# Block 2 of a two-block kernel: attention's scratch memory taken apart from linear attention's, and its steps released earlier

## The reference, cut to what matters

```python
px, pc = split_cols(hx @ w_in + b_in), split_cols(hc @ w_in + b_in)   # tokens, context
ya_x = conv_module(*px[0:3], dw_w, dw_b, ln_g, ln_b, w_conv_out)      # 31 taps
yb_x, yb_c = gla_branch(px[3:9], pc[3:9], ..., need_ctx)              # gated linear attention
yc_x, yc_c = attn_branch(px[9:13], pc[9:13], q_norm_g, k_norm_g, w_attn_out, need_ctx)
xs = xs + gate_x * ((sigmoid(p[13]) * ya + sigmoid(p[14]) * yb + sigmoid(p[15]) * yc) @ w_out)

def gqa_attend(q, k, v):            # 8 query heads, 2 key heads, 64 wide
    s = einsum('bqkgd,bskd->bkgqs', q, k) * 64 ** -0.5
    return einsum('bkgqs,bskd->bqkgd', softmax(s, axis=-1), v)
```

## Time and profile before

| | |
|---|---|
| median of 3 runs | 1394.38 us |
| the profiled execution's own time | 1394.86 us |
| its span | 1393.5 us |
| PE busy | 1314.5 us (94%) |
| DVE busy | 870.2 us (62%) |
| ACT busy | 584.5 us (42%) |
| POOL busy | 281.6 us (20%) |
| chain that ended last: PE, DVE, issue, POOL | 74%, 10%, 10%, 4% |

### The profile page before, as it was taken

The page is one execution under the profiler, slowest core; times in us unless marked ns, Lnnn a source line. Parts: engine busy times, 40 slices in busy tenths (PEclk is TensorE's granted clock), DMA queues, the critical chain, the costliest instruction groups (busy, mean ns, idle before and its releaser), DMA issues.

```text
span 1393.5 us, 18891 instructions
## 1 busy us (share of the span) xinstructions
PE 1314.5 (94%) x7490; PEld 1037.0 (74%) x7490; DVE 870.2 (62%) x1496; ACT 584.5 (42%) x967; POOL 281.6 (20%) x217
## 2 busy tenths in 40 slices
PE   7999987999979999997999999999999998799998
PEld 5777766777757777775777887777898876488876
DVE  4795756685677542499996522424576688845553
ACT  3444533344454445222434532323463663356442
POOL 0110013100033322247000011311252142201112
PEclk9999998999999999999999999999999999989999
DMA  7674465363433411121111222223553333123451
GB/s 250 226 269 143 143 242 190 129 226 136 164 109 109 152 51 61 46 75 61 62 46 46 64 88 91 91 91 93 165 166 99 103 106 105 47 85 118 145 176 66
DMA packets 49192, 168.46 MB, mean 121 GB/s; under 512 B 5862, under 2 KB 7078, under 8 KB 48848
## 3 DMA queue, kind: packets, MB, share of 16 engines
q1 hardware_dynamic: 49104, 167.26, 36.0%
HBM read 166.19 MB, written 1.05 MB: 120 GB/s over the span
## 4 chain that ended last, share of the span: by engine, by line
PE 74%; DVE 10%; issue 10%; POOL 4%; ACT 1%; DMA 1%; SPq 0%; POOLq 0%; DVEq 0%; ACTq 0%
PE bank L1493 16%; PE bank L1494 15%; PE bank L1495 15%; PE bank L1412 3%; PE bank L1806 3%; DVE conv_val L2555 3%; PE bank L1511 3%; PE bank L1512 2%; PE bank L1513 2%; DVE w_lo L2235 2%; PE bank L1573 2%; PE bank L1781 1%; PE bank L1536 1%; PE bank L1426 1%; PE bank L1742 1%
## 5 line engine op out<-in xcount | busy, mean ns | idle before, releaser
L1493 PE MATMUL bank<-w_hi,x_hi 128*128 128x512 f32 (+4 forms) x1120 | 466.4, 416 | 18.1 <-DVE x_lo L2245 12.3
L2235 DVE TENSOR_TENSOR w_lo<-w_raw,w_hi 128x1024 fp32r<-128x1024 f32 (+3 forms) x264 | 322.4, 1224 | 252.3 <-ACT w_hi L1843 252.2
L1843 ACT ACTIVATE w_hi<-w_raw 128x1024 fp32r<-128x1024 f32 (+3 forms) x264 | 269.8, 1026 | 442.6 <-PE bank L1495 249.9
L1494 PE MATMUL bank<-w_lo,x_hi 128*128 128x512 f32 (+4 forms) x1120 | 436.4, 390 | 0.0
L1495 PE MATMUL bank<-w_hi,x_lo 128*128 128x512 f32 (+4 forms) x1120 | 435.7, 389 | 0.0
L1493 PEld LDWEIGHTS bank<-w_hi,x_hi 128*128 128x128 f32 x1120 | 215.8, 193 | 72.0 <-DVE x_lo L2245 15.5
L1495 PEld LDWEIGHTS bank<-w_hi,x_lo 128*128 128x128 f32 x1120 | 214.0, 191 | 46.4
L1494 PEld LDWEIGHTS bank<-w_lo,x_hi 128*128 128x128 f32 x1120 | 215.3, 192 | 38.7
L2555 DVE SCALAR_TENSOR_TENSOR conv_val<-conv_u,par,conv_val 128x512 f32<-128x512 f32 (+1 forms) x240 | 150.2, 674 | 0.0
L2875 POOL TENSOR_TENSOR merged<-merged,sigma 128x512 f32<-128x512 f32 x24 | 37.4, 1585 | 178.6 <-DVE sigma L2597 178.6
L1511 PE MATMUL bank<-x_hi,w_hi 128*128 128x512 f32 (+1 forms) x192 | 67.0, 349 | 0.5 <-ACT conv_val L2045 0.5
(11 more groups left out here) (330 smaller groups left out, 1727.2 us busy)
## 6 DMA issues: line engine op xcount, KB each, us to landing
w_raw<-in_w SPq DMA_DIRECT2D x172, 512.0 KB, 3.5
w_raw<-in_wm SPq DMA_DIRECT2D x48, 512.0 KB, 5.1
w_raw<-in_wo SPq DMA_DIRECT2D x40, 512.0 KB, 3.5
w_raw<-in_wy_gla SPq DMA_DIRECT2D x8, 512.0 KB, 3.5
w_raw<-in_wy_att SPq DMA_DIRECT2D x8, 512.0 KB, 3.5
w_raw<-in_wy_conv SPq DMA_DIRECT2D x8, 512.0 KB, 3.5
w_raw<-in_w SPq DMA_DIRECT2D x8, 460.0 KB, 5.5
w_raw<-in_w SPq DMA_DIRECT2D x12, 288.0 KB, 2.8
```

The lines of the kernel that those rows point to most:

```text
L1493: mm(out, xh[:, q, col], hi[:, kk, 0:w], start=kp == 0 and kk == 0 and not with_bias, stop=False)
L1494: mm(out, xh[:, q, col], lo[:, kk, 0:w], start=False, stop=False)
L1843: do(hi, raw, ACT.Copy).then_inc(sem["cut_hi"], 1)
L2235: v.tensor_tensor(lo, raw, hi.bitcast(F32), ALU.subtract).then_inc(sem["cut_lo"], 1)
```

## The change

The scratch memory of attention is laid out anew. `att_k_t`, `att_stat` and the third probability buffer (`att_p_2`) get places that linear attention does not use. `att_q_t` is gone: the turned queries are written over the queries in `att_q`, a column block at a time. The two other probability buffers and the two buffers of turned probabilities stay in shared places in the first layer; in the last layer they lie in the context half of `x_hi2` and `x_lo2` (`lent_prob`, `lent_turned`), which is free once the projection `GV` of tile 3 has read it. The order of `AFTER` follows: keys and queries are turned as soon as their norms are there. The scores of the first layer still wait for `gla_o` of tile 1; those of the last layer wait only for `GV`. No arithmetic is added or removed.

```diff
-    "ak_flip": lambda l: normed(l, "k") + [("gla_o", l, 1), ("gla_st", l, 0, 3, 1)],
+    "ak_flip": lambda l: normed(l, "k"),
-    "aq_flip": lambda l, j: normed(l, "q") + [("gla_o", l, 1)],
+    "aq_flip": lambda l, j: normed(l, "q"),
-    "a_s": lambda l, qt, j: [("aq_act", l, 2), ("aq_dve", l, 3), ("ak_t", l)],
+    "a_s": lambda l, qt, j: [("aq_act", l, 2), ("aq_dve", l, 3), ("ak_t", l)] + over_attention(l),
...
+def over_attention(l):
+    return [("gla_o", l, 1), ("gla_st", l, 0, 3, 1)] if l < LAYERS - 1 else [("project", "in2", l, GV, NP - 1, 3)]
...
+            b.lent = [sb(n, [P, KD, 2 * S], F32, scope) for n in ("lent_prob", "lent_turned")]
...
-            b.aq_t, b.ak_t = sb("att_q_t", [P, AH // 2, 512], F32, scope), sb("att_k_t", [P, 512], F32, scope)
-            b.aprob, b.astat = sb("att_p", [P, 3, 512], F32, scope), sb("att_stat", [P, 2, 24], F32, scope)
+            sb("beside", [P, 5, 512], F32, scope)
+            b.aprob = sb("att_p", [P, 2, 512], F32, scope)
...
+        b.ak_t, b.aprob_2, b.astat = sb("att_k_t", [P, 512]), sb("att_p_2", [P, 512]), sb("att_stat", [P, 2, 24])
...
+    def prob_home(self, l, qt, j):
+        b, p = self.b, self.slot("a_prob", l, qt, j)[0]
+        if p == 2:
+            return b.aprob_2.rearrange("p (a b) -> p a b", a=2)
+        if l == LAYERS - 1:
+            return b.lent[0][:, 4 + 2 * p:6 + 2 * p, S:2 * S]
+        return b.aprob[:, p].rearrange("p (a b) -> p a b", a=2)
...
-                         b.aq_t[rows, h % 4, qt * P:(qt + 1) * P], b.ak_t[rows, k0:k0 + keys], start=True, stop=True)
+                         b.aq[rows, qt, h % 4 * P:(h % 4 + 1) * P], b.ak_t[rows, k0:k0 + keys], start=True, stop=True)
...
-        act.wait_ge("gla_o", l, 1)
         act.wait_ge("aq_flip", l, j)
-        do(b.aq_t[:, j, 0:n], ps[:, 0:n], ACT.Copy, scale=HD ** -0.5).then_inc(sem["aq_act"], 1)
+        do(b.aq[:, 0:n // P, j * P:(j + 1) * P], ps[:, 0:n].rearrange("p (t q) -> p t q", q=P), ACT.Copy, scale=HD ** -0.5).then_inc(sem["aq_act"], 1)
...
         act.wait_ge("a_max", l, qt, j)
+        if l < LAYERS - 1:
+            act.wait_ge("gla_o", l, 1)
+            act.wait_ge("gla_st", l, 0, 3, 1)
+        else:
+            act.wait_ge("project", "in2", l, GV, NP - 1, 3)
```

More of the change, by code:

```diff
@@ L946, in before_flip, with over_operand @@
     earlier = branch_before(l, i)
-    return [("gla_o", l, 1) if earlier is None else ("project", f"y{earlier}", l, 1, 1, tiles_of(l)[-1])]
+    if earlier is None:
+        return over_operand(l)
+    return [("project", f"y{earlier}", l, 1, 1, tiles_of(l)[-1])]
+def over_operand(l):
+    return [("gla_o", l, 1)] if l < LAYERS - 1 else [("project", "in2", l, GV, NP - 1, 3)]
+def over_attention(l):
+    return [("gla_o", l, 1), ("gla_st", l, 0, 3, 1)] if l < LAYERS - 1 else [("project", "in2", l, GV, NP - 1, 3)]
 def normed(l, what):
@@ L1293, in second_begin @@
         b.acc = sb("merged", [P, 4, D])
+        with ExitStack() as scope:
+            b.lent = [sb(n, [P, KD, 2 * S], F32, scope) for n in ("lent_prob", "lent_turned")]
         b.xh, b.xl = sb("x_hi2", [P, KD, 2 * S], F32R), sb("x_lo2", [P, KD, 2 * S], F32R)
@@ L1786, in a_flip @@
         i, before = slot("aux", "a_flip", l, qt, j)
-        prob = b.aprob[:, slot("a_prob", l, qt, j)[0]]
+        prob = k.prob_home(l, qt, j)
         pe.wait_ge("a_exp", l, qt, j)
         pe.wait_ge(*(before or ()))
-        flips(k.bank[i], [prob[:, c * P:(c + 1) * P] for c in range(4)]).then_inc(sem["a_flip"], 1)
+        flips(k.bank[i], [prob[:, c // 2, c % 2 * P:(c % 2 + 1) * P] for c in range(4)]).then_inc(sem["a_flip"], 1)
     def a_v(l, qt, j):
         i, before = slot("sum2", l, qt)
-        turned = b.aprob_t[:, slot("a_prob_t", l, qt, j)[0]]
+        turned = k.turned_home(l, qt, j)
         key_tiles = EVERY if qt in X_TILES else C_TILES
@@ L1871, in flip_hi @@
             earlier = branch_before(l, int(source[1]))
-            act.wait_ge(*(("gla_o", l, 1) if earlier is None else ("project", f"y{earlier}", l, 1, 1, tiles_of(l)[-1])))
+            act.wait_ge(*over_operand(l)[0] if earlier is None else ("project", f"y{earlier}", l, 1, 1, tiles_of(l)[-1]))
         elif source == "merged":
@@ L2181, in a_exp @@
             h = places(qt, j)[g]
-            ins = do(b.aprob[:, p, g * keys:(g + 1) * keys], ps[:, g * keys:(g + 1) * keys], ACT.Exp,
+            ins = do(prob[:, g * halves:(g + 1) * halves, :],
+                     ps[:, g * keys:(g + 1) * keys].rearrange("p (a b) -> p a b", a=halves), ACT.Exp,
                      bias=stat[:, h:h + 1], accum_out=stat[:, AH + h:AH + h + 1])
@@ L2190, in a_t_act @@
         act.wait_ge(*(before or ()))
-        do(b.aprob_t[:, p, :], ps[:, :], ACT.Copy).then_inc(sem["a_t_act"], 1)
+        do(k.turned_home(l, qt, j), ps[:, :].rearrange("p (a b) -> p a b", a=2), ACT.Copy).then_inc(sem["a_t_act"], 1)
     def gate_rows(l, s, c):
@@ L2711, in ak_t @@
         ps = k.bank[slot("aux", "ak_flip", l)[0]]
-        dve.wait_ge("gla_o", l, 1)
-        dve.wait_ge("gla_st", l, 0, 3, 1)
         dve.wait_ge("ak_flip", l)
@@ L2719, in aq_dve @@
         ps = k.bank[slot("aux", "aq_flip", l, j)[0]]
[L2720 removed]
         dve.wait_ge("aq_flip", l, j)
[L2722 removed]
+        v.tensor_scalar(b.aq[:, 0:n // P, j * P:(j + 1) * P], ps[:, 0:n].rearrange("p (t q) -> p t q", q=P), HD ** -0.5, None,
+                        ALU.mult).then_inc(sem["aq_dve"], 1)
     def a_max(l, qt, j):
```

13 lines of the change are left out of this document (9 added, 4 removed).

## The result

| kernel | median | lowest to highest | runs |
|---|---|---|---|
| before | 1394.23 us | 1392.82 to 1395.92 | 18 |
| changed | 1397.82 us | 1395.82 to 1401.81 | 18 |

The ratio is 1.0025, with a 95% interval of 1.0018 to 1.0031: the change costs 3.6 us, where 1392.5 was predicted. The time lies just above the stated range (1388.0 to 1397.5), and the sign was missed.

The account below looks back on a forecast made before the run. PE was taken as the bound, busy 1314.5 of 1393.5 us. Terms +0.3 - 0.9 - 0.25 - 1.0 = -1.85 from 1394.86 gave 1393.0; that execution lay 0.5 above the median, so 1392.5 us was predicted, range 1388.0 to 1397.5.

Parts of the forecast that it names:

- No product is added or removed, so the change can pay only in two ways: Whole kernel: gain only from PE standing idle for less time or its clock being low for less time.
- What it gets done earlier pushes the projections back by the same amount: Last layer, start of attention: PE has enough to do until 1190.7 us anyway, so earlier scores and transpositions delay projections equally.
- First layer, +0.3: First-layer gating: 7.92 us hole stays, about 1 us wait for tile 1 replaces one of 0.85; +0.3 us, bounds 0 and +3.
- Gate sums, -0.9: Last layer, 4.5 us wait for `gla_la`: 1.1 us of transpositions fills it, 0.2 us delay comes in; -0.9 us.
- Start of attention, -0.25: Last layer, `gla_o` to `y1`: eight waits of together 8.45 us instead of 8.7; -0.25 us, bounds -4 and +4.
- the new wait behind `conv_dev`: Last layer, start of attention: map 5 waits 1.7 us for `conv_dev`, which frees the bank of the mean.
- The clock, -1.0: Start of attention, last layer: low clock for some 11 us instead of 13.8, costing 4.0 us instead of 5.0; -1.0 us.
- The bounds of 5.0 to either side: Clock at the start of attention: -5.0 us if it does not fall, +5.0 if it falls sooner.
- Everything else costs nothing: Rest of the kernel: same copied elements in another shape, scores read as many columns, weight cuts stay ahead of use; 0.
- The clock low for longer: Rival, chance 0.14: clock falls at the first waits around `gla_o` and stays low until `y1`; 1398.5 us.
- The first layer's hole: Rival, chance 0.12: tile 1's gating behind a slowed norm makes the query blocks wait, 3 us more; 1395.5 us.

Follow-up runs that it names:

- e9: Changed kernel, but in the last layer only the keys are turned early; queries, scores and `y1`'s operand wait for `gla_o` of tile 1: 1390.3 us, ratio 0.9978.
- e10: Changed kernel, but the last layer's scores are released behind the last state step instead of behind the projection of `gla_v`: 1394.0 us, ratio 0.9999.
- e4: Changed kernel, but last-layer scores and `y1`'s operand wait for `gla_o` of tile 1 as before; keys and queries still turned early: 1397.6 us, ratio 1.0022.
- e5: The changed kernel run again as it is, for a second trace: 1397.0 us, ratio 1.0020.
- e3: Changed kernel with the last layer's order as before (keys, queries and scores behind `gla_o` of tile 1), first layer as changed: 1394.4 us, ratio 1.0001.
- e12: e4 with the first layer as before, so only the last layer's keys and queries are turned early: 1387.4 us, ratio 0.9961.
- e14: e4 plus thirteen useless products (3.0 us of PE work) in a last-layer projection ahead of its holes: 1390.5 us, ratio 0.9975.
- e16: e12 plus two useless products (0.5 us of PE work) in a last-layer projection ahead of its holes: 1395.9 us, ratio 1.0006.
- e1: Changed kernel's new places with the old order of transpositions and scores in both layers: 1394.5 us, ratio 1.0000.
- e7: Changed kernel plus twelve useless products (2.8 us of PE work) in the last layer's `y2`, ahead of the last holes: 1397.9 us, ratio 1.0028.
- e15: Changed kernel plus thirteen useless products (3.0 us of PE work) in a last-layer projection ahead of its holes: 1402.8 us, ratio 1.0063.
- e2: Changed kernel with the first layer's keys and queries turned only behind `gla_o` of tile 1 and the state, as before: 1395.3 us, ratio 1.0018.
- e8: e1 plus two useless products (0.5 us of PE work) in the last layer's `y2`, ahead of the last holes: 1396.3 us, ratio 1.0010.

## Why the prediction was wrong, step by step

**"No product is added or removed, so the change can pay only in two ways": this step failed first.** It put PE's own work at no change. The number of products is the same, their time is not. From A to B PE's work grew by 2.5 us: 1.5 for the state steps, 0.4 for `gla_q_t` by `gla_k_t`, 0.4 for turning probabilities, and some 0.2 net from the rest. "What it gets done earlier pushes the projections back by the same amount" was therefore wrong: scores and the keys' transposition put among the projections part steps that overlapped as neighbours. e9 and e10 show that for the state steps, and e10, which moves only the scores, brings `gla_q_t` by `gla_k_t` back to 3.3 us of 3.7, as expected; for the other items it is read from the traces, not tested.

**First layer, +0.3:** the hole is 7.6 us and the one after it 1.3, instead of 7.9, 0.85 and 0.5. Tile 1's gating did go behind the norm, but PE did not wait for it, where about 1 us was forecast; the 1.3 is a wait for a copy of `att_q` by DVE. From 503 to 802 us the layer costs 0.4 us more without a fall of the clock (e4, e5), near the term. What I did not have is the clock's fall at 538 us: 1.5 us more in six of the ten traces with this first layer, in none of the eight with the old one. e3 shows that the median doesn't feel it by itself; of the traces with the changed first layer, those without the fall lost 2.5 to 4.2 us more to the clock ahead of 503 us than those with it.

**Gate sums, -0.9:** 1.65 and 1.82, together 3.5 us of 4.5: -1.0. Right for the idle time. What the sum did not have is the clock behind this place: it is low for 10.2 us in the changed kernel, 6.8 before, which costs 1.3 us more and takes back the gain.

**Start of attention, -0.25:** seven waits of 7.9 us instead of eight of 8.7, so -0.8, with the new wait behind `conv_dev` at 1.5 (1.7 forecast). Right in kind. What the sum left out is that the order of the scores alone can take much more off: scores behind the states (e10) bring the idle time from A to B from 11.4 to 8.2 us.

**The clock, -1.0: the size failed, and clock terms were missing elsewhere.** The forecast was for the start of attention alone: low for 11 us instead of 13.8. It is low for 13.7 us in both kernels (from 1213.5 us before, from 1217.1 in the changed one), and it costs 4.9 us instead of 5.1: -0.2. The clock behind the gate sums (+1.3) and the fall in the first layer (+1.5) had no term at all; from A to B the clock took 1.1 us more, with the first layer's fall 2.6. I worked with one trace and took its clock as a property of the order. The same order costs 4.8 or 11.6 us of clock, by when its holes come (e4, e12, e14, e16); even the last holes, which the change doesn't touch, are worth 2.4 us (e1, e7). The bounds of 5.0 to either side held for the changed kernel, but e15's trace goes beyond them: its clock took 5.8 us more than before, 5.9 of it at this place. The point in them was not to be had from one trace.

**"Everything else costs nothing":** right for the copies and the lent places (e1).

**The rivals.** The clock low for longer (1398.5) came nearest in time, by luck: its place and mechanism are not in the changed kernel, where the clock falls at 1217.1, behind both `gla_o`, for no longer than before. Nearest to it come e15, low from 1208.3 us, in the second `gla_o`, for 27.3 us, and e10, from 1209.9 for 20.5. The first layer's hole (1395.5) did not grow. The measured +3.6 us are, by the two profiled executions (+3.5), 1.9 ahead of A, and between A and B 2.5 of work and 1.1 of clock less 2.1 of idle time saved; B to C gives nothing; by the ratios, nothing for the first layer alone (e3), 0.0018 for the last one alone (e2). The 1.9 ahead of A and the 1.1 of clock are what these two executions had; by e1 and e8 such items change from one execution to the next with the order unchanged.

What stays open: why the changed kernel as a whole stands at a bad moment in nearly all its runs (1395.8 us at the least, where the kernel before has 1395.9 at the most in the same comparison), and so how much of the 3.6 us belongs to its order and how much to that moment. No version was run that only parts the pairs.

## What to carry to other kernels

Work that fills a hole is not free because it was "only moved": see which small products stood side by side on different rows, and keep them so. Where PE's holes are 1 to 3 us long, the clock's cost depends on the moment at which they come as much as on their length; before a change of order is judged by 0.3%, put half a microsecond and then three of useless work ahead of the place and look at the spread. The version found here, the new places with keys and queries of the last layer turned early and the rest of the order as before (e12), beats the kernel before by 0.4% and the changed one by 0.6% (by the ratios), but e16 shows that this gain is as fragile as the loss; e14 gives 0.25% with 3 us of useless work in it.

## What was not expected of the hardware

- The clock falls where PE is busy for all of 50 us (granted clock 0.97 from 500 to 550 us in the changed kernel and e3, 1.00 in e4, with the same order there). Just ahead of the fall, from 529.0 to 537.7 us, PE has the small products of linear attention, between the projections.
- The same three holes of 1.2, 1.1 and 1.6 us are followed by a low clock in some executions and not in others (0.91 and 1.00), at a price of 2.4 us.
- 3.0 us of added work made a kernel 7.0 us faster (e4 to e14); 0.5 us made another 8.5 us slower (e12 to e16); each pair was run on two chips.
- Sixteen products of 64x64 weights take 0.68 us as neighbours on different rows (one pair, the first of the own tiles, takes 1.08), 1.09 on the same rows, and eight alone take 0.65.
